# Order inside a stick-breaking attention step: transposes, value products, scores; turned-weight copies ahead of the sigmoids

## The reference

```python
z = q @ k.T * scale                      # a tile of 128 queries, 128 or 256 keys
mask = k_pos < q_pos
log_beta = log_sigmoid(z)
log_keep = where(mask, log_sigmoid(-z), 0)
tail = reversed_cumsum(log_keep) - log_keep
w = where(mask, exp(log_beta + tail), 0)
y = w @ v
```

## Time and profile before

| | |
|---|---|
| Median of 3 runs | 2780.32 us (2779.09 to 2784.46) |
| Profiled execution, its own time | 2781.0 us |
| Span of the profiled execution | 2779.2 us |
| PE busy, matmuls | 2644.3 us (95%), 14804 instructions |
| PE busy, weight loads | 2147.7 us (77%) |
| DVE busy | 1677.7 us (60%) |
| ACT busy | 1384.8 us (50%) |
| Mean granted PE clock | 0.984 |
| Chain that ended last | PE 82%, DVE 8%, ACT 6%, issue 4% |

### The profile page before, as it was taken

One profiled execution on the slowest core, in us unless ns is written; L12 is line 12 of the kernel. 1 busy time (PEld: TensorE's weight loads), 2 busy tenths in 40 slices (PEclk: granted clock), 3 DMA queues, 4 the chain that ended last, 5 costly groups with the idle time before them and its releaser, 6 DMA issues.

```text
span 2779.2 us, 40667 instructions
## 1 busy us (share of the span) xinstructions
PE 2644.3 (95%) x14804; PEld 2147.7 (77%) x14804; DVE 1677.7 (60%) x2560; ACT 1384.8 (50%) x2245; POOL 94.8 (3%) x104
## 2 busy tenths in 40 slices
PE   8999999998999999899999998999999899999998
PEld 7768888676888888688876777777777678667997
DVE  5754445756999998354645545553454456456766
ACT  5644335654777776434345344432333544455654
POOL 2000001000000000000000100000000110010000
PEclk9999999999999999899999999999999899999999
DMA  7439795435999997322321213544552234334464
GB/s 227 135 121 275 244 304 161 132 117 176 322 333 322 320 327 267 95 69 69 87 83 58 74 56 99 151 145 136 152 157 79 82 108 121 94 104 129 144 184 142
DMA packets 352458, 444.87 MB, mean 160 GB/s; under 512 B 19616, under 2 KB 197920, under 8 KB 352288
## 3 DMA queue, kind: packets, MB, share of 16 engines
q1 hardware_dynamic: 349792, 435.44, 49.6%
q0 software_dynamic: 2208, 6.79, 0.8%
q10 hardware_dynamic: 288, 0.36, 0.0%
HBM read 441.48 MB, written 1.05 MB: 159 GB/s over the span
## 4 chain that ended last, share of the span: by engine, by line
PE 82%; DVE 8%; ACT 6%; issue 4%; POOL 0%; DVEq 0%; ACTq 0%; POOLq 0%
PE ps L2441 21%; PE ps L2489 17%; PE ps L2428 15%; PE ps L2502 8%; PE ps L2493 4%; PE ps L2510 2%; PE ps L2813 2%; PE ps L2824 2%; ACT w_hi L1060 2%; PE ps L2844 2%; PE ps L2700 2%; PE ps L2810 1%; PE ps L2528 1%; DVE w_lo L1579 1%; PE ps L2382 1%
## 5 line engine op out<-in xcount | busy, mean ns | idle before, releaser
L1579 DVE TENSOR_TENSOR w_lo<-raw,w_hi 128x1024 fp32r<-128x1024 f32 (+1 forms) x578 | 683.6, 1199 | 493.8 <-ACT w_hi L1060 431.3
L1060 ACT ACTIVATE w_hi<-raw 128x1024 fp32r<-128x1024 f32 (+1 forms) x578 | 585.3, 1029 | 251.5 <-PE ps L2441 120.3
L2489 PE MATMUL ps<-w_hi,h_hi 128*128 128x512 f32 (+1 forms) x992 | 403.6, 409 | 11.5 <-DVE h_lo L2051 3.9
L2489 PE MATMUL ps<-w_hi,h_lo 128*128 128x512 f32 (+1 forms) x992 | 379.5, 385 | 0.0
L2428 PE MATMUL ps<-h_hi,w_hi 128*128 128x256 f32 (+1 forms) x1008 | 301.4, 324 | 16.4 <-ACT w_hi L1060 11.3
L2502 PE MATMUL ps<-w_lo,h_hi 128*128 128x512 f32 (+1 forms) x992 | 297.6, 384 | 0.0
L2428 PE MATMUL ps<-h_lo,w_hi 128*128 128x256 f32 (+1 forms) x1008 | 296.7, 320 | 0.0
L2489 PEld LDWEIGHTS ps<-w_hi,h_hi 128*128 128x128 f32 x992 | 187.2, 189 | 70.2 <-issue 33.2
L2428 PEld LDWEIGHTS ps<-h_hi,w_hi 128*128 128x128 f32 x1008 | 192.2, 191 | 49.4 <-ACT w_hi L1060 15.3
L2502 PEld LDWEIGHTS ps<-w_lo,h_hi 128*128 128x128 f32 x992 | 183.0, 188 | 39.5
L2489 PEld LDWEIGHTS ps<-w_hi,h_lo 128*128 128x128 f32 x992 | 187.2, 189 | 29.2 <-issue 1.0
(11 more groups left out here) (312 smaller groups left out, 4209.8 us busy)
## 6 DMA issues: line engine op xcount, KB each, us to landing
raw<-in_w_in SPq DMA_DIRECT2D x196, 512.0 KB, 3.7
arena<-in_w_mod SPq DMA_DIRECT2D x96, 512.0 KB, 5.2
raw<-in_w_up SPq DMA_DIRECT2D x88, 512.0 KB, 4.4
raw<-in_w_gu_exp SPq DMA_DIRECT2D x64, 512.0 KB, 5.4
arena<-in_w_gu_exp SPq DMA_DIRECT2D x64, 512.0 KB, 4.9
arena<-in_w_gu_exp SPq DMA_DIRECT2D x64, 384.0 KB, 3.9
arena<-in_w_dn_exp SPq DMA_DIRECT2D x48, 512.0 KB, 6.3
raw<-in_w_gu_dense SPq DMA_DIRECT2D x44, 512.0 KB, 7.6
```

The costliest lines, as they stand in the source:

```text
L1060: nc.scalar.activation(w_hi[:, half, 0:n], place[:, 0:n], ACT.Copy).then_inc(seg.sig.hi_ready, 1)
L1579: nc.vector.tensor_tensor(w_lo[:, half, 0:n], place[:, 0:n], w_hi[:, half, 0:n].bitcast(F32), ALU.subtract).then_inc(seg.sig.lo_ready, 1)
L2489: ins = mm(ps[:, 2 * h + p % 2, 0:width], x[:, k + c, p * P:(p + 1) * P], wh[:, c * width:(c + 1) * width], start=opens and c == 0 and x i ...
```

## The change

The branch for `soft` becomes the only one, for both engines. For the stick-breaking steps PE now does the transposes of item k-2, the value products of items k-4 and k-3, the scores of items k and k+1; ACT now copies the turned weights of item k-2, then does the sigmoids of item k, then the output. DVE's order, the waits, the buffers and the number of instructions stay.

```diff
@@ ACT, attend @@
-                if st.mode == "soft" and 2 <= k <= n + 1:
+                if 2 <= k <= n + 1:
                     turned_weights(k - 2)
                 if k < n:
                     weights(k)
-                if st.mode != "soft" and 2 <= k <= n + 1:
-                    turned_weights(k - 2)
                 if k >= 3:
                     output(k - 3)
@@ PE, attend @@
-                if st.mode == "soft":
-                    if 2 <= k <= n + 1:
-                        turn(k - 2)
-                    if k % 2 == 0 and k >= 4:
-                        pair_gather(k - 4)
-                    if k % 2 == 0 and k < n:
-                        pair_scores(k)
-                    return
+                if 2 <= k <= n + 1:
+                    turn(k - 2)
+                if k % 2 == 0 and k >= 4:
+                    pair_gather(k - 4)
                 if k % 2 == 0 and k < n:
                     pair_scores(k)
-                if k % 2 == 0 and k >= 4:
-                    pair_gather(k - 4)
-                if 2 <= k <= n + 1:
-                    turn(k - 2)
```

## The result

| | before | after |
|---|---|---|
| Median of the runs | 2780.32 us | 2792.61 us (5 runs, 2788.67 to 2794.12) |
| Ratio to before, 95% interval | | 1.0038 [1.0027, 1.0049] |
| Profiled execution, span | 2779.2 us | 2790.8 us |
| Stretch of layer 0, length | 49.73 us | 56.27 us |
| Stretch of layer 1, length | 49.71 us | 54.78 us |

Slower by 0.38%, or 10.6 us by the ratio (12.3 by the medians); 8.2 were forecast. The direction and the mechanism are as forecast; the median itself lies 1.1 us above the top of the forecast's range (2791.5), the ratio's 2790.9 just inside it. The length of a stretch is the distance from PE's first load for the scores of step 0 to its first load for the value products of step 18; this measure is used throughout. The two stretches grew by 6.54 and 5.07 us, 11.6 together, which is what the span grew by.

A forecast was written before the change was run, and what follows sets the result against it. PE was taken to bound both stick-breaking stretches (busy 47.3 of 50.4 us). Steps 4, 8, 12, 16 cost 0.90, 1.29, 1.47, 0.44: 4.10 us a layer, 8.2 in all, giving 2788.5 us; range 2780 to 2791.5.

The forecast's parts named there:

- first step: PE, steps 4, 8, 12: transposes waiting for DVE's multiplication stand first, three blocks follow, 1.19 us; step 4 alone 0.79 later.
- late scores: Scores last in steps 2, 6, 10, 14 start DVE's bounding later: 0.26, 0.66, 0.85 us, step 14 taken as 10.
- As PE runs these blocks without a gap: Single steps: the scores, now last, end where the step's last block, the transpose, ended before; step 10: 80.31 against 79.46.
- The copy: ACT's copy leaves the chain between sigmoids and split, saving 0.15 us of issue, covered by ACT's wait for the bounding.
- what is late next: Double steps: DVE's bounding, 1.5 to 2 us late, then ACT's work; PE has a unit or two meanwhile, cost nothing.
- Rival C: Double steps' waits merge into some 2 us, clock halves; 1.9 us each, six times, 11.4 on top, 2800 us; chance 0.03.
- a clock below 1.00 in them: Sign that the forecast is wrong: granted clock under 1.00 in the two stick-breaking stretches.
- Rivals A and B: A: multiplication early enough in double steps, 2774.7 us, chance 0.05; B: no measurable change, 2780 to 2785.5 us, chance 0.29.

The follow-up runs named there:

- E2: PE's new order alone, ACT's order as in the kernel before; ratio to the kernel before 1.0038.
- E3: The changed kernel with PE's new order only in steps 4, 8, 12, 16, scores first in 2, 6, 10, 14; ratio to before 1.0031.
- E4: The changed kernel with PE's new order only in steps 2, 6, 10, 14, scores first in 4, 8, 12, 16; ratio to before 1.0.
- E5: The changed kernel profiled again without edit; ratio to before 1.0039, layer 0's stretch 53.14 us at full clock.
- E9: E3 plus 14 unread transposes of the identity in PE's wait of steps 4, 8, 12; ratio to before 1.0025, 2789.73 us.
- E10: The kernel before, with DVE doing the first of a unit's two stick steps ahead of its split of unit j+2; ratio to before 0.9978.
- E7: The kernel before with ACT's new order, and DVE's first of two stick steps ahead of its split of unit j+2; 2773.78 us, ratio 0.9973.

## Why the prediction was right, point by point

**The mechanism.** As put in its first step: PE's first wait in steps 4, 8 and 12 is for the multiplication, the other two blocks stand behind it, and 1.16 us follow (1.19 forecast). E2, E3 and E4 put the loss on PE's order in just these steps.

**The terms.** At full clock, in E5's layer 0, read as the growth of the distance from one double step to the next:

| | step 4 | step 8 | step 12 | step 16 | stretch |
|---|---|---|---|---|---|
| forecast, us | 0.90 | 1.29 | 1.47 | 0.44 | 4.10 |
| measured, us | 0.72 | 1.08 | 1.24 | 0.37 | 3.41 |
| of it late scores, forecast | 0.26 | 0.66 | 0.85 | 0.85 | 2.62 |
| of it late scores, measured | 0.11 | 0.48 | 0.65 | 0.66 | 1.90 |

Step 8's row of E5 shows it: multiplication, then three blocks, then the next unit (before, relative to the stretch's start, it came at 23.39, here at 25.19).

```profile
73.16 0.43 DVE L2164 TENSOR_TENSOR arena<-arena 128x256 f32<-128x256 f32 x1
73.64 0.20 PEld L2822 LDWEIGHTS ps<-ident,arena 128*128 128x128 f32 x2 [2.40 <-DVE arena L2164]
...
74.01 0.20 PEld L2842 LDWEIGHTS ps<-arena 128*64 128x64 f32 x4 [0.17 <-issue]
...
74.38 0.30 PEld L2811 LDWEIGHTS ps<-arena 64*128 64x128 f32 x4 [0.17 <-issue]
...
74.80 0.19 PEld L2487 LDWEIGHTS ps<-w_hi,h_hi 128*128 128x128 f32 x1
```

The late scores are how much later the bounding in the single step before it (2, 6, 10, 14) starts, counted from the unit behind the previous double step (in step 2 from the stretch's start). They hold the whole difference: each was sized 0.15 to 0.20 us too high, since I took the end of the scores from the end of the old transposes. In step 6 the scores end at 68.59, 7.32 us after the next unit's start behind step 4; the old transposes ended 7.50 after it.

```profile
67.89 0.70 PE L2811 MATMUL ps<-arena 64*128 64x256 f32 x4
...
68.64 0.42 DVE L2141 SCALAR_TENSOR_TENSOR arena<-ps,strict 128x256 f32<-128x256 f32 x1 [0.41 <-PE ps L2811]
```

"As PE runs these blocks without a gap" held.

**Which term carries it.** The forecast split its 4.1 us into 1.5 without the late scores and 2.6 with them. Measured it is 1.5 and 1.9, so the first size held. The copy was worth what it was priced at: from bounding to split it is 1.25 us instead of 1.40. "I cost it at nothing", said of what is late next, held too: in step 6's row above DVE has caught up and itself waits 0.41 us for PE, and in E9, where only the double steps have late scores, the bounding of items 6, 10 and 14 starts as long after the unit before (6.87, 6.69 and 6.68 us) as in the kernel before (6.89, 6.71 and 6.71). E3 and E4 must not be read as the two terms one by one, as each leaves ACT's copy beside an order of PE that the change doesn't have there.

**Rival C came too.** I gave half clock 0.03, since the stretches showed 1.00 with the old idle times in them, and named a clock below 1.00 in them as a sign of being wrong. That sign appeared, in both stretches. The profiles with PE waits of 2.2 to 2.4 us (the change, E2, E3, E5) have spells after nine of 24 such waits (one of them, in step 8 of layer 1 of E3, twice as long as the others); the eight with shorter waits or with filled ones have none. So rival C did not replace the forecast, it came on top of it, at times: some 1.6 us a spell (1.9 was priced), three spells in one profile and one in the next. The Trainium skill's rule that activity releases a throttle which is otherwise the default (TensorE: Matmul & The Clock Gate, Part 1) agrees with what the filler did: transposes of the identity in the wait kept 1.00 in twelve of twelve waits. Before, the 1.19 and the 0.62 us were parted by a block of scores; now 2.23 us stand in one piece. I had forecast that length (some 2 us), but looked for its price only inside the stretches. Elsewhere the trace of the kernel before has a piece like it:

```profile
447.33 0.14 PEld L2656 LDWEIGHTS ps<-ident,arena 128*128 128x128 f32 x1 [2.26 <-issue]
```

```profile
446.00:449.00 3.00, 1.09 (x7) 0.81 (x8) 1.26 (x5) 2.71 (x10) 1.52 (x2) 1.00 0.01 5
449.60:452.90 3.30, 3.30 (x16) 3.27 (x16) 2.71 (x5) 1.03 (x3) 2.20 (x2) 0.50 0.20 34
```

Half clock follows, and does so at this place in ten of the twelve profiles. PE is less busy around it than in the stretches, so this doesn't give the chance there, but it speaks against 0.03.

Rivals A and B are out: the multiplication was not early (59.84 against the 59.12 needed), and nothing later took the delay in.

**Sum.** Order 6.8 us (8.2 forecast) and clock 1.6 to 4.8 us (none forecast) make 8.4 to 11.6; 10.6 was measured. The total came close partly by luck: late scores priced 1.4 us too high and a clock priced at nothing offset each other.

What stays open: which of the long waits brings a spell, since step 4 of layer 1 was followed by one in all four profiles, but the same step of layer 0 in one of them only; and 1 to 3 us of the difference in the times of the filled kernels, which their stretches don't show and which is about the width of the intervals.

## What to carry to other kernels

An in-order engine that waits for several partners should have the latest wait last, behind all it can do meanwhile; an order that is right for one attention (softmax, whose probabilities come early) need not be right for another whose chain is longer. Before blocks are reordered around a wait, ask what the awaited engine has in front of its answer: here one DVE step moved ahead of a split that nobody needed yet removed the wait and gained 6 us by itself (E10), 7 with the change's order on ACT (E7), two results whose intervals overlap. And count the length of the longest idle piece of PE as well as the sum, because merged waits can cost clock that separate ones did not. When half of a change is taken back to price the other half, check that the mixture has no wait of its own, as E3 had on ACT.

## What the runs showed of the hardware that was not expected

PE idle for 2.2 to 2.4 us at a time, in a stretch in which it is otherwise busy, was followed in nine of 24 cases by a spell at 1.2 GHz; idle pieces of at most 1.34 us within the stretches never were. (All are gaps between PE's loads; its matmuls stood still 1.7 to 2.0 us in the long ones.) The same program had three spells in one execution and one in another, which is a source of scatter between executions by itself. And 14 transposes of 128x128 whose result nobody reads, put into the wait, cost at most 0.1 us a stretch (53.25 and 53.19 against 53.14) and kept the clock at 2.4 GHz.
